# Sums of squares of the queries half a block later, and an inner dimension cut into two chunks of eleven tiles

## The chip, the cores and the metric

One core of one Trainium2 chip. The time is the device time of one execution in microseconds (us); less is better. Five engines run in parallel, each through its own instruction queue in order, and meet only at semaphores: TensorE (PE, with its weight loads PEld), VectorE (DVE), ScalarE (ACT), GpSimd (POOL) and SyncE (SP). In this kernel SP issues plain DMAs, POOL issues plain ones and ones that add to what is there.

## What is computed

Two layers of a streaming encoder on 16 + 512 tokens (528 columns), model width 1024, inner width 2816. Each layer: a SwiGLU, a mixer (a convolution branch and a windowed attention with 16 query and 4 key heads of 64, gated and summed), and a second SwiGLU.

```python
x = x + 0.5 * (silu(gate) * up) @ w_out          # gate | up = rms_norm(x) @ w_in, FFN 1
p = rms_norm(x) @ w_in                           # conv inputs | q | k | v | gates
q, k = rms_norm(q, q_norm), rms_norm(k, k_norm)  # over the 64 of each head
y_b = window_sink_attention(q, k, v, sinks) @ attn_w_out
x = x + (sigmoid(g_a) * conv_module(p) + sigmoid(g_b) * y_b) @ w_out
x = x + 0.5 * (silu(gate) * up) @ w_out          # FFN 2
```

## The kernel before, in words

**Precision.** Every weight and every activation is split in two float32r parts, high and low, and each product is made of three matmuls (high by high, high by low, low by high). The high part of a weight is a copy by ACT; the low part is either a subtraction by DVE, or ACT writes the negated high part and POOL adds the weights to it with an accumulating DMA.

**Four FFN stages** (s = 0 to 3, two in each layer; 22 inner tiles of 128 each; s = 3 runs on 512 columns, the others on two halves of 264). The input product of one inner tile, a "pair" of gate and up, is made by a seven-product scheme: P1 to P7, twelve matmuls each. TensorE's order for pair j is P1, P2, P7 of the pair before, P5, P6, P4 of the pair before, P3. DVE and ACT combine the products (L1532 to L1567) into `hh` and `hl`, the inner tiles.

**Chunks and output products.** `CHUNKS` cuts the 22 inner tiles into 7, 7 and 8. After the last pair of a chunk TensorE runs the output products: for each of 8 outputs m, the chunk's inner tiles times one block of `w_out`, accumulated in PSUM (`out_products`, L1127). Since P7 and P4 of the last pair still have to follow, the first block is begun with one inner tile, then comes P7, a second tile, P4 and the rest. The block of weights for an output goes through three slots in rotation: SP loads it (`load_out`, L544) when the slot's last user is done, ACT makes the high part (`out_hi`, L696), DVE the low part (`out_lo`, L1463), and TensorE waits for `ob_lo`. DVE then scales the output out of PSUM (L1634) and adds it to the residual (L1638). In the last chunk of a stage, what follows on the residual is done output by output as well: in stage 1 the operands of the next seven-product scheme (`x7_parts` on ACT, `x7_operands` on DVE, which end with L1396), in stages 0 and 2 the operands of the mixer.

**The slots.** The units that hold weights are shared by pairs, output blocks and mixer blocks; `freed`, `out_freed` and `mix_freed` say which product has to be over before a unit is loaded again. Pairs alternate between two sets of units, and the output blocks use the set that the last pair did not.

**The mixer.** Per layer four groups g of 11 blocks (two of queries, one of keys and values, eight others that fill TensorE while attention is prepared), each of 8 x 3 matmuls over the tokens (`products`, L1061). At the end of block 3 stands `head_stats`: 9 small products (8 in the second layer) of the squared queries with a two-column matrix (L1224), the keys' sums of squares (L1227), and transposes of the values (L1230 to L1233). ACT then takes the roots (`head_std`: L903 for the queries, L904 for the keys) and copies the transposed values (L906 to L908, which release `v_ready`); DVE takes reciprocals and scales the keys (`head_rms`, L1711 to L1723); SP copies the keys to the other half of the partitions (L570), and TensorE makes the first scores after block 5 (L1252). The queries' factors are first needed by `row_max`, which DVE reaches in block 5.

Of the kernel before, what the change touches and what calls it, by code (L numbers as in the profile page):

```python
# [29 lines left out]
P = 128  # L30
# [8 lines left out]
CHUNKS = ((0, 7), (7, 14), (14, KF))  # L39
# [46 lines left out]
OUT_UNITS = ((0, 2, 4), (8, 10, 12))  # L86
# [86 lines left out]
def tensor_order():  # L173

    for s in range(STAGES):
        for c, (a, b) in enumerate(CHUNKS):
            for j in range(s * KF + a, s * KF + b):
                yield "P1", j
                yield "P2", j
                if j > s * KF + a:  # L180
                    yield "P7", j - 1
                yield "P5", j
                yield "P6", j
                if j > s * KF + a:
# [4 lines left out]
            for m in range(KD):  # L189
                yield "out", s, c, m  # L190
        if s % 2 == 0:
            for n in range(NBLK):
                yield "mix", s // 2, n
# [5 lines left out]
def freed(j, part):  # L199

    s, c, i = chunk_of(j)
    product = {"A": "P2", "S12": "P6", "S43": "P7", "A22": "P4"}[part]
    if i > 1:
        return USED[product, j - 2]
    after_mixer = c == 0 and begins(s)
    if after_mixer and s == 0:
        return 0
    if after_mixer:
        m = {"A": 6, "S12": 7, "S43": 5, "A22": 4}[part]
        return USED["mix", s // 2, B_MO + m] if i or part == "A22" else 0  # L210
# [5 lines left out]
    return USED["out", s, c, {"A": 6, "S12": 7, "S43": 5}[part]]  # L216
# [32 lines left out]
def build(nc, x, params, qk_gain, sinks, pairs, outs7, outs8, mixes, out):  # L249
# [7 lines left out]
    with ctx:  # L257
# [47 lines left out]
        hh, hl = sb("hh", [P, KD, NT], F32R, ffn), sb("hl", [P, KD, NT], F32R, ffn)  # L305
# [112 lines left out]
        def out_block(s, c, m):  # L418

            last = s * KF + CHUNKS[c][1] - 1  # L420
            return (s * len(CHUNKS) + c) * KD + m + 1, OUT_UNITS[1 - REGION[last]][m % 3], CHUNKS[c][1] - CHUNKS[c][0]

        def out_load(s, c, m):

            return (s * len(CHUNKS) + c) * (3 if m % 3 < 2 else 2) + m // 3 + 1
# [46 lines left out]
        qk_stat = sem("qk_stat")  # L472
# [47 lines left out]
        def _(sp):  # L520
# [17 lines left out]
            def load_out(s, c, m):  # L538
                count, u, k = out_block(s, c, m)
                sp.wait_ge(blk_used, out_freed(s, c, m))  # L540
                n = count - 1 - (s * len(CHUNKS) + c) * KD
                i = s * len(CHUNKS) + c
                src = outs8[s * KD + n, :, :, :] if k == KD else outs7[(i - s) * KD + n, :, :, :]
                sp.dma_start(units(f32_units, u, 2)[:, 0:k, :], src).then_inc(ob_in[m % 3], 16)  # L544

            def stage(s):
                for c, (ta, tb) in enumerate(CHUNKS):
                    for t in range(ta, tb):
                        j = s * KF + t
                        if j + 2 < run_of(j)[1]:  # L550
                            load_pair(j + 2)
                        if t == tb - 2:
                            load_out(s, c, 0)
                        if t == tb - 1:
                            load_out(s, c, 1)
                            load_out(s, c, 2)
                    for m in range(KD - 3):
                        load_out(s, c, m + 3)
# [86 lines left out]
        def _(act):  # L645
# [45 lines left out]
            def out_hi(s, c, m):  # L691
                if m >= KD:
# [84 lines left out]
            def ffn(l, f):  # L777
                s = 2 * l + f
                last_chunk = len(CHUNKS) - 1
                for c, (ta, tb) in enumerate(CHUNKS):  # L780
# [56 lines left out]
                    for m in range(KD):  # L837
                        if m:
                            out_hi(s, c, m + 2)
                        if m == KD - 1 and more:  # L840
                            base_hi(j1 + 1)
                        if c == last_chunk:
                            if f == 0 and m == 0:
                                act.wait_ge(lay, l + 1)
                            if f == 0 and m in (5, 7):
                                neg(l, B_MIX + (m - 5) // 2)
                            act.wait_ge(res_done, out_block(s, c, m)[0])
                            outer(l, m, 1 if f == 0 else 3, R_MIX if f == 0 else None)
# [52 lines left out]
            def head_std(l, g):  # L901
                act.wait_ge(qk_stat, l * GROUPS + g + 1)
                func(qstd[:, lead(l):, :], qss[:, lead(l):, :], ACT.Sqrt, bias=eps64[:, :]).then_inc(qstd_ready, 1)  # L903
# [4 lines left out]
                func(vm[:, HD:P], pov[0:MB, 128:128 + HD], ACT.Copy).then_inc(v_ready, 1)  # L908

# [19 lines left out]
            for l in range(DEPTH):  # L929
                ffn(l, 0)  # L930

                for g in range(GROUPS):
# [23 lines left out]
                    h(4)  # L956
                    fill_tanh(l, g, 4)
# [86 lines left out]
        def _(pe):  # L1044
# [72 lines left out]
            def out_products(s, c, m, ks):  # L1117
                count, u, n = out_block(s, c, m)
                hi, lo = units(hi_units, u, 2), units(lo_units, u, 2)
                j0 = s * KF + CHUNKS[c][0]  # L1120
                post = s == STAGES - 1
                for k in ks:
                    if m == 0 and k >= n - 2:
                        pe.wait_ge(h_lo, j0 + k + 1)
                    for p, (a, b) in enumerate(((hi, hh), (hi, hl), (lo, hh))):
                        for h, t, width in pieces(post):
                            ins = mm(po[:, 2 * ps(m) + h, 0:width], a[:, k, :], b[:, k, t:t + width],  # L1127
                                     start=k == 0 and p == 0, stop=k == n - 1 and p == 2, skip_group_check=True)
                if n - 1 in ks:
                    ins.then_inc(blk_used, 1)  # L1130

            def ffn(l, f):
                s, which = 2 * l + f, 2 * f
                for c, (ta, tb) in enumerate(CHUNKS):
# [61 lines left out]
                    n = tb - ta  # L1196
                    pe.wait_ge(ob_lo, before_c + 1)
# [6 lines left out]
                    out_products(s, c, 0, range(2, n))  # L1204
                    for m in range(1, KD):
                        pe.wait_ge(ob_lo, before_c + m + 1)
                        if m > 1:
                            pe.wait_ge(ffn_taken, before_c + m - 1)
                        out_products(s, c, m, range(n))
# [7 lines left out]
            def head_stats(l, g):  # L1217
# [11 lines left out]
                for c in range(NCH):  # L1229
# [4 lines left out]
                    .then_inc(qk_stat, 1)  # L1234

# [56 lines left out]
            def mixer_in(l):  # L1292
                for g in range(GROUPS):
# [7 lines left out]
                    mids = {7: do(lambda: S(1)), 8: do(lambda: V(0), lambda: T(1)),  # L1301
# [67 lines left out]
        def _(dve):  # L1369
# [88 lines left out]
            def out_lo(s, c, m):  # L1458
                if m >= KD:
                    return  # L1460
# [109 lines left out]
            def ffn(l, f):  # L1570
                s = 2 * l + f
                post = s == STAGES - 1
                for c, (ta, tb) in enumerate(CHUNKS):
# [47 lines left out]
                    for m in range(KD):  # L1621
# [8 lines left out]
                        count = out_block(s, c, m)[0]  # L1630
                        dve.wait_ge(blk_used, USED["out", s, c, m])
# [76 lines left out]
            def head_rms(l, g):  # L1708
                n = l * GROUPS + g
                dve.wait_ge(qstd_ready, n + 1)  # L1710
                nc.vector.reciprocal(qrms[:, :, :], qstd[:, :, :]).then_inc(qrms_ready, 1)  # L1711
                dve.wait_ge(kstd_ready, n + 1)
                dve.wait_ge(qrms_ready, n + 1)
                ts(nqrms[:, :, :], qrms[:, :, :], -1.0, None, ALU.mult)
# [9 lines left out]
                    .then_inc(kn_ready, 1)  # L1724

# [46 lines left out]
            for l in range(DEPTH):  # L1772
# [10 lines left out]
                for g in range(GROUPS):  # L1783
                    for i in range(GB_N):
# [98 lines left out]
def laid_out(inputs):  # L1883
# [12 lines left out]
    for l in range(DEPTH):  # L1896
        for name in ("ffn1", "ffn2"):
# [3 lines left out]
            for a, b in CHUNKS:  # L1901
                outs += [block(f"{name}_w_out", l, a, b - a, ((m * P, P),)) for m in range(KD)]
# [10 lines left out]
        "outs7": np.stack([b for b in outs if b.shape[1] < KD]),  # L1913
        "outs8": np.stack([b for b in outs if b.shape[1] == KD]),
# [18 lines left out]
```

## Time and profile before

| | |
|---|---|
| median of 3 runs | 2423.99 us (2418.34 to 2425.91) |
| profiled execution: time | 2424.94 us |
| profiled execution: span | 2423.1 us |
| mean granted TensorE clock over the span | 0.992 |
| busy: PE, DVE, ACT, POOL | 98%, 71%, 50%, 14% |

The views that follow are the page's list of busy engines and of DMA issues, the list of TensorE's waits, sums over stretches (with the granted clock), the chain of waits and the order of time. "Busy" counts a matmul from its start to its end; since the next one starts before that, TensorE can lose time without being idle, and the starts in the order of time have to be compared. A matmul over 264 columns that follows another densely starts some 0.122 us after it, and ends 0.28 us after its start.

### The profile page before, as it was taken

To read this page: it belongs to the slowest core of one execution; us is meant where nothing else is said; L and a number is where in the kernel's file an instruction comes from. 1 tells how busy PE (TensorE), PEld (TensorE's weight loads), DVE (VectorE), ACT (ScalarE), POOL (GpSimd) and SP (SyncE) were. 2 spreads that over 40 slices of the span, in tenths; PEclk is the share of its full clock that TensorE was granted. 3 is DMA by queue.
4 is the path that set the end of the run, shared out by engine and by line. 5 is a ranking of instruction groups with operands and counts; after the bars stand their busy time and mean duration, and the time that the engine had idled before them with its cause. 6 is when DMAs were issued, how large, how long until landed. Compare 5 with 4: busy or idle time off the path is not lost.

```text
span 2423.1 us, 43031 instructions
## 1 busy us (share of the span) xinstructions
PE 2378.2 (98%) x17637; PEld 2236.9 (92%) x17637; DVE 1720.2 (71%) x2740; ACT 1222.0 (50%) x1991; POOL 345.3 (14%) x454
## 2 busy tenths in 40 slices
PE   7999999999999999999999999999999999999999
PEld 6999999999999999999989999998888777889897
DVE  8766664798886477667787676647888855867584
ACT  7554543443444375546565455543434454746371
POOL 1010101121112210101001101011211122101010
PEclk9999999999999999999999999999999999999999
DMA  6655646666667966556546556466676698657472
GB/s 172 154 136 147 154 111 140 145 146 144 139 141 172 209 134 152 145 144 155 146 106 161 141 145 151 112 146 145 145 153 144 130 217 191 144 143 175 116 176 92
DMA packets 106756, 358.69 MB, mean 148 GB/s; under 512 B 12096, under 2 KB 12096, under 8 KB 106560
## 3 DMA queue, kind: packets, MB, share of 16 engines
q0 software_dynamic: 64080, 210.53, 43.0%
q1 hardware_dynamic: 42112, 145.08, 19.8%
q8 instruction: 140, 2.29, 0.4%
q14 instruction: 56, 0.46, 0.1%
q10 hardware_dynamic: 368, 0.33, 0.0%
HBM read 351.41 MB, written 2.10 MB: 146 GB/s over the span
## 4 chain that ended last, share of the span: by engine, by line
PE 87%; DVE 4%; DMA 4%; ACT 3%; issue 2%; POOL 0%; DVEq 0%; ACTq 0%; SPq 0%
PE po L1061 30%; PE po L1078 20%; PE po L1127 19%; PE ptr L1078 8%; PE pov L1078 5%; DMA wla<-in_mixes 1%; PE pov L1289 1%; PE pov L1287 1%; PE ptr L1268 1%; PE pstat L1252 1%; DMA raw<-in_pairs 1%; PE pov L1224 1%; DVE rms L1520 0%; PE pstat L1227 0%; DMA wha<-in_mixes 0%
## 5 line engine op out<-in xcount | busy, mean ns | idle before, releaser
L1061 PE MATMUL po<-xh,wha 128*128 128x264 f32 (+1 forms) x1408 | 348.2, 314 | 4.5 <-DMA wla<-in_mixes 3.9
L1061 PE MATMUL po<-xl,wha 128*128 128x264 f32 (+1 forms) x1408 | 339.2, 308 | 0.0
L1061 PE MATMUL po<-xh,wla 128*128 128x264 f32 (+1 forms) x1408 | 338.4, 307 | 0.0
L1670 DVE SCALAR_TENSOR_TENSOR cv<-ub,lp,cv 128x528 f32<-128x528 f32 (+1 forms) x480 | 333.3, 754 | 1.7
L1061 PEld LDWEIGHTS po<-xh,wha 128*128 128x128 f32 x1408 | 230.3, 191 | 23.3 <-DVE t L1873 3.5
L1078 PE MATMUL po<-x7h,wha 128*128 128x264 f32 (+1 forms) x844 | 241.1, 286 | 4.1 <-ACT tmp L702 1.6
L1078 PE MATMUL po<-x7l,wha 128*128 128x264 f32 (+1 forms) x844 | 240.3, 285 | 0.0
L1061 PEld LDWEIGHTS po<-xh,wla 128*128 128x128 f32 x1408 | 229.7, 191 | 11.3
L1078 PE MATMUL po<-x7h,wla 128*128 128x264 f32 (+1 forms) x844 | 239.8, 284 | 0.0
L1061 PEld LDWEIGHTS po<-xl,wha 128*128 128x128 f32 x1408 | 229.7, 191 | 10.3
L658 ACT ACTIVATE wla<-wha 128x1024 fp32r<-128x1024 f32 x136 | 143.1, 1054 | 162.2 <-DMA wha<-in_mixes 162.1
L1078 PE MATMUL po<-x7h,whb 128*128 128x264 f32 (+1 forms) x692 | 197.8, 286 | 11.8 <-DMA wlb<-in_pairs 4.6
L1078 PE MATMUL po<-x7l,whb 128*128 128x264 f32 (+1 forms) x692 | 197.0, 285 | 0.0
L1078 PE MATMUL po<-x7h,wlb 128*128 128x264 f32 (+1 forms) x692 | 196.6, 284 | 0.0
L607 POOL DMA_DIRECT2D wha<-in_mixes x136 | 75.8, 560 | 674.8 <-PE po L1061 612.5
L1078 PEld LDWEIGHTS po<-x7h,wha 128*128 128x128 f32 x844 | 159.1, 189 | 5.6 <-issue 2.8
L1127 PE MATMUL po<-hh,wha 128*128 128x264 f32 (+1 forms) x688 | 161.7, 303 | 0.0
L1127 PE MATMUL po<-hh,wla 128*128 128x264 f32 (+1 forms) x688 | 161.3, 303 | 0.0
L1127 PE MATMUL po<-hl,wha 128*128 128x264 f32 (+1 forms) x688 | 161.2, 302 | 0.0
L1078 PEld LDWEIGHTS po<-x7l,wha 128*128 128x128 f32 x844 | 159.6, 189 | 0.0
L1078 PEld LDWEIGHTS po<-x7h,wla 128*128 128x128 f32 x844 | 159.3, 189 | 0.0
L611 POOL DMA_DIRECT2D wla<-in_mixes x136 | 122.4, 900 | 171.1 <-ACT wla L658 169.9
(247 smaller groups left out, 6297.0 us busy)
## 6 DMA issues: line engine op xcount, KB each, us to landing
wha<-in_mixes POOLq DMA_DIRECT2D x136, 512.0 KB, 4.4
wla<-in_mixes POOLq DMA_DIRECT2D x136, 512.0 KB, 6.4
raw<-in_pairs SPq DMA_DIRECT2D x88, 768.0 KB, 5.1
wlb<-in_pairs POOLq DMA_DIRECT2D x45, 512.0 KB, 7.6
raw<-in_pairs SPq DMA_DIRECT2D x88, 256.0 KB, 5.9
wla<-in_pairs POOLq DMA_DIRECT2D x87, 256.0 KB, 6.7
wfa<-in_outs SPq DMA_DIRECT2D x48, 448.0 KB, 3.4
wla<-in_pairs POOLq DMA_DIRECT2D x41, 512.0 KB, 8.2
```

The source lines that it names most:

```text
L607: pool.dma_start(mix_units(hi_units, n), mixes[l * NBLK + n, :, :, :]).then_inc(w_hi[n % 4], 16)
L611: pool.dma_start(mix_units(lo_units, n), mixes[l * NBLK + n, :, :, :], accum_op=ALU.add)\
L658: func(mix_units(lo_units, n), mix_units(hi_units, n).bitcast(F32), ACT.Copy, scale=-1.0)\
L1061: ins = mm(po[:, 2 * out_slot + h, 0:width], w[:, k, :], v[:, k, t:t + width], start=begin and k == 0 and p == 0, stop=last and k == kt - ...
L1078: ins = mm(bank, a[:, kp, :], b[:, kp, cols7], start=begin and kp == 0 and p == 0, stop=kp == KP - 1 and p == 2, skip_group_check=True)
L1127: ins = mm(po[:, 2 * ps(m) + h, 0:width], a[:, k, :], b[:, k, t:t + width], start=k == 0 and p == 0, stop=k == n - 1 and p == 2, skip_grou ...
L1224: mm(qss[:, pos, :], qsq[:, tok0(pos):tok0(pos) + CHUNK, :].rearrange("p n j -> p (n j)"), halves[:, :], start=True, stop=True)
L1252: ins = mm(score(i, h), q[r, :], kw[r, c:c + WK], start=True, stop=True)
L1268: tr(ptr[:, h * P:(h + 1) * P], pw[:, (b + 1) % 2, at:at + WIN], ident[:, :])
L1287: mm(dst[h * HD:(h + 1) * HD], vw[:, pos - 1, :], cut(pt[:, h, :]), start=True, stop=False, skip_group_check=True)
L1289: mm(dst, vm[:, :], cut(ptm[:, :]), start=pos == 0, stop=True, skip_group_check=True).then_inc(pv_done, 1)
L1670: stt(cv[:, j, a:], u, w, cv[:, j, a:], ALU.mult, ALU.add).then_inc(conv_step, 1)
```

## The change

The inner tiles are cut into two chunks of 11 in place of 7, 7 and 8, so each output is added to the residual twice per stage and not three times. An output's 11 tiles of weights no longer fit a slot of 8; they come as two blocks of 6 and 5 tiles, 16 blocks per chunk through the same three slots, in the order of units 2, 4, 0 where it was 0, 2, 4. The inner tiles `hh`, `hl` grow from 8 to 11 tiles, and the room for them comes from the scratch space that the software DMA queue reserves (`dynamic_dma_scratch_size=4096`). In the mixer the queries' small products, their root and their reciprocal leave `head_stats`, `head_std` and `head_rms`: TensorE makes them in the middle of block 4 after `v_ready`, ACT takes the root before that block's tanh, DVE the reciprocal after that block was taken.

```diff
-CHUNKS = ((0, 7), (7, 14), (14, KF))
+CHUNKS = ((0, 11), (11, KF))
+CHUNK_T = 11
+BLOCKS = ((0, 6), (6, CHUNK_T))
+NB = KD * len(BLOCKS)
-OUT_UNITS = ((0, 2, 4), (8, 10, 12))
+OUT_UNITS = ((2, 4, 0), (10, 12, 8))
...
 def out_freed(s, c, m):
     if m > 2:
         return USED["out", s, c, m - 3]
-    return USED[("P2", "P6", "P7")[m], s * KF + CHUNKS[c][1] - 2]
+    return USED[("P6", "P7", "P2")[m], s * KF + CHUNKS[c][1] - 2]
...
-    return USED["out", 2 * l, len(CHUNKS) - 1, n + 4]
+    return USED["out", 2 * l, len(CHUNKS) - 1, NB - 4 + n]
...
                     for m in range(KD):
                         if m:
-                            out_hi(s, c, m + 2)
+                            out_hi(s, c, 2 * m + 2)
+                        out_hi(s, c, 2 * m + 3)
...
             def head_std(l, g):
                 act.wait_ge(qk_stat, l * GROUPS + g + 1)
-                func(qstd[:, lead(l):, :], qss[:, lead(l):, :], ACT.Sqrt, bias=eps64[:, :]).then_inc(qstd_ready, 1)
...
+            def query_std(l, g):
+                act.wait_ge(q_stat, l * GROUPS + g + 1)
+                func(qstd[:, lead(l):, :], qss[:, lead(l):, :], ACT.Sqrt, bias=eps64[:, :]).then_inc(qstd_ready, 1)
...
                     h(4)
+                    query_std(l, g)
                     fill_tanh(l, g, 4)
...
+                    for b in range(NB):
+                        pe.wait_ge(ob_lo, before_b + b + 1)
+                        m = b // 2
+                        if m > 1 and b % 2 == 0:
                             pe.wait_ge(ffn_taken, before_c + m - 1)
+                        out_products(s, c, b, range(0 if b else 2, out_block(s, c, b)[2]))
...
                 pe.wait_ge(ksq_ready, l * GROUPS + g + 1)
-                pe.wait_ge(qsq_ready, 2 * (l * GROUPS + g) + 2)
                 pe.wait_ge(o_lo, (l * GROUPS + g) * NBAT + 1)
-                for pos in range(lead(l), NPOS):
-                    mm(qss[:, pos, :], qsq[:, tok0(pos):tok0(pos) + CHUNK, :].rearrange("p n j -> p (n j)"),
-                       halves[:, :], start=True, stop=True)
...
+            def query_stats(l, g):
+                pe.wait_ge(qsq_ready, 2 * (l * GROUPS + g) + 2)
+                pe.wait_ge(v_ready, l * GROUPS + g + 1)
+                for pos in range(lead(l), NPOS):
+                    ins = mm(qss[:, pos, :], qsq[:, tok0(pos):tok0(pos) + CHUNK, :].rearrange("p n j -> p (n j)"),
+                             halves[:, :], start=True, stop=True)
+                ins.then_inc(q_stat, 1)
...
-                    mids = {7: do(lambda: S(1)), 8: do(lambda: V(0), lambda: T(1)),
+                    mids = {4: do(lambda: query_stats(l, g)), 7: do(lambda: S(1)), 8: do(lambda: V(0), lambda: T(1)),
...
                         if m:
-                            out_lo(s, c, m + 2)
+                            out_lo(s, c, 2 * m + 2)
+                        out_lo(s, c, 2 * m + 3)
...
+            def query_rms(l, g):
+                n = l * GROUPS + g
+                dve.wait_ge(qstd_ready, n + 1)
+                nc.vector.reciprocal(qrms[:, :, :], qstd[:, :, :]).then_inc(qrms_ready, 1)
+                dve.wait_ge(qrms_ready, n + 1)
+                ts(nqrms[:, :, :], qrms[:, :, :], -1.0, None, ALU.mult)
...
                         if i == 3:
                             head_rms(l, g)
+                        if i == 4:
+                            query_rms(l, g)
...
-    nc = bacc.Bacc("TRN2", target_bir_lowering=False, num_devices=1)
+    nc = bacc.Bacc("TRN2", target_bir_lowering=False, num_devices=1, dynamic_dma_scratch_size=4096)
```

## Rows read from the trace of the kernel before

**Rows 1.** The page: each engine's busy time, share of the span, instructions.
```profile
PE 2378.2 (98%) x17637; PEld 2236.9 (92%) x17637; DVE 1720.2 (71%) x2740; ACT 1222.0 (50%) x1991; POOL 345.3 (14%) x454
```
**Rows 2.** TensorE's waits, whole span: us in total, times, longest us.
```profile
PE po L1078 <- ACT tmp L707: 2.6, 4, 0.9
...
PE po L1061 <- DMA wla<-in_mixes: 3.9, 4, 1.5
...
PE pstat L1252 <- DMA kw<-kw: 0.8, 1, 0.8
```
**Rows 3.** Sums over 10 us (a group's statistics; last: stage 2): busy (x), PEclk, DMA.
```profile
413.00:423.00 10.00, 10.00 (x72) 9.30 (x71) 6.11 (x7) 4.52 (x8) 1.44 (x2) 0.83 0.65 132
497.00:507.00 10.00, 10.00 (x84) 9.30 (x83) 6.48 (x8) 5.83 (x10) 1.44 (x2) 1.00 0.61 124
...
663.80:673.80 10.00, 10.00 (x59) 8.57 (x58) 5.12 (x6) 5.83 (x10) 1.44 (x2) 0.66 0.59 120
...
1236.00:1246.00 10.00, 7.17 (x31) 6.34 (x31) 8.15 (x13) 7.04 (x10) 0.86 (x1) 0.67 0.29 52
```
**Rows 4.** The same sums for TensorE alone, at either clock, after the first group's statistics.
```profile
417.00:420.00 3.00, 3.00 (x14) 0.50 0.91 173
420.40:423.40 3.00, 3.00 (x27) 1.00 0.02 4
```
**Rows 5.** Order of time, first group's statistics: start us, us, engine, line, [idle before].
```profile
413.05 2.07 PE L1224 MATMUL pov<-halves,pw 128*128 128x2 f32 x18
...
415.04 1.10 PE L1227 MATMUL pstat<-t,ones 64*64 64x264 f32 x4
...
416.68 0.22 PE L1233 MATMUL pov<-ident,kvp 64*32 64x64 f32 x1
...
417.24 0.27 DVE L1711 RECIPROCAL qrms<-qstd 128x18 f32<-128x18 f32 x1 [3.29 <-ACT qstd L903]
...
418.27 0.20 ACT L908 ACTIVATE vm<-pov 32x64 f32<-32x64 f32 x1
```
**Rows 6.** Order of time: second layer's query products; two idle stretches of TensorE.
```profile
1871.04 1.84 PE L1224 MATMUL pov<-halves,pw 128*128 128x2 f32 x16
...
2097.31 0.39 PE L1078 MATMUL po<-x7h,whb 128*128 128x256 f32 x1 [1.75 <-ACT tmp L702]
...
1240.27 0.59 PE L1078 MATMUL ptr<-x7h,wha 128*128 128x264 f32 x1 [2.29 <-DVE x7l L1419]
```
**Rows 7.** Order of time, end of stage 0's first chunk; last row: of its third.
```profile
98.96 1.08 DVE L1463 TENSOR_TENSOR wla<-wfa,wha 128x896 fp32r<-128x896 f32 x1
...
99.53 0.41 PE L1127 MATMUL po<-hh,wha 128*128 128x264 f32 x2
99.63 0.94 ACT L696 ACTIVATE wha<-wfa 128x896 fp32r<-128x896 f32 x1
...
100.53 0.36 PE L1078 MATMUL ptr<-x7h,whb 128*128 128x264 f32 x1
...
338.82 0.36 PE L1078 MATMUL ptr<-x7h,wha 128*128 128x264 f32 x1 [0.24 <-DVE tmp L1536]
```
**Rows 8.** DMA issues (KB, us to landing); and output products in the chain of waits.
```profile
raw<-in_pairs SPq DMA_DIRECT2D x88, 768.0 KB, 5.1
...
wfa<-in_outs SPq DMA_DIRECT2D x48, 448.0 KB, 3.4
...
104.66 39.46 PE po L1127 x324
```
**Rows 9.** Order of time, last outputs of stage 1 and start of stage 2.
```profile
1221.94 0.49 PE L1127 MATMUL po<-hh,whb 128*128 128x264 f32 x2 [0.48 <-DVE t L1634]
...
1233.74 0.28 PE L1078 MATMUL ptr<-x7h,wha 128*128 128x264 f32 x1
...
1235.83 0.70 DVE L1634 SCALAR_TENSOR_TENSOR t<-po,rms 128x528 f32<-128x528 f32 x1
...
1241.65 0.70 DVE L1396 TENSOR_TENSOR pw<-pw 128x528 f32<-128x528 f32 x1
```

More of the change, by code:

```diff
@@ L188, in tensor_order @@
             yield "P4", s * KF + b - 1
-            for m in range(KD):
-                yield "out", s, c, m
+            for b in range(NB):
+                yield "out", s, c, b
         if s % 2 == 0:
@@ L215, in freed @@
     s, c, _ = chunk_of(j - 2)
-    return USED["out", s, c, {"A": 6, "S12": 7, "S43": 5}[part]]
+    return USED["out", s, c, {"A": NB - 2, "S12": NB - 1, "S43": NB - 3}[part]]
 def out_freed(s, c, m):
@@ L304, in build @@
         raw = sb("raw", [P, 2, 4 * KP, P], at=ffn)
-        hh, hl = sb("hh", [P, KD, NT], F32R, ffn), sb("hl", [P, KD, NT], F32R, ffn)
+        hh, hl = sb("hh", [P, CHUNK_T, NT], F32R, ffn), sb("hl", [P, CHUNK_T, NT], F32R, ffn)
         ffn.close()
@@ L420, in out_block @@
             last = s * KF + CHUNKS[c][1] - 1
-            return (s * len(CHUNKS) + c) * KD + m + 1, OUT_UNITS[1 - REGION[last]][m % 3], CHUNKS[c][1] - CHUNKS[c][0]
+            a, b = BLOCKS[m % 2]
+            return (s * len(CHUNKS) + c) * NB + m + 1, OUT_UNITS[1 - REGION[last]][m % 3], b - a
         def out_load(s, c, m):
-            return (s * len(CHUNKS) + c) * (3 if m % 3 < 2 else 2) + m // 3 + 1
+            return (s * len(CHUNKS) + c) * len(range(m % 3, NB, 3)) + m // 3 + 1
         def mix_units(bufs, n):
@@ L471, in build @@
         qsq_ready, ksq_ready = sem("qsq_ready"), sem("ksq_ready")
-        qk_stat = sem("qk_stat")
+        qk_stat, q_stat = sem("qk_stat"), sem("q_stat")
         qstd_ready, kstd_ready, v_ready = sem("qstd_ready"), sem("kstd_ready"), sem("v_ready")
@@ L556, in stage @@
                             load_out(s, c, 2)
-                    for m in range(KD - 3):
-                        load_out(s, c, m + 3)
+                    for b in range(NB - 3):
+                        load_out(s, c, b + 3)
             load_x(0)
@@ L691, in out_hi @@
             def out_hi(s, c, m):
-                if m >= KD:
+                if m >= NB:
                     return
@@ L846, in ffn @@
                                 neg(l, B_MIX + (m - 5) // 2)
-                            act.wait_ge(res_done, out_block(s, c, m)[0])
+                            act.wait_ge(res_done, (s * len(CHUNKS) + c) * KD + m + 1)
                             outer(l, m, 1 if f == 0 else 3, R_MIX if f == 0 else None)
@@ L1115, in last_product, with out_products @@
                 seventh("P4", j, x_bank(j), begin=False)
-            def out_products(s, c, m, ks):
-                count, u, n = out_block(s, c, m)
+            def out_products(s, c, b, ks):
+                _, u, size = out_block(s, c, b)
                 hi, lo = units(hi_units, u, 2), units(lo_units, u, 2)
                 j0 = s * KF + CHUNKS[c][0]
+                m, k0 = b // 2, BLOCKS[b % 2][0]
                 post = s == STAGES - 1
                 for k in ks:
[L1123 to L1129, printed above, removed]
+                    t = k0 + k
+                    if m == 0 and t >= CHUNK_T - 2:
+                        pe.wait_ge(h_lo, j0 + t + 1)
+                    for p, (w, v) in enumerate(((hi, hh), (hi, hl), (lo, hh))):
+                        for h, x, width in pieces(post):
+                            ins = mm(po[:, 2 * ps(m) + h, 0:width], w[:, k, :], v[:, t, x:x + width],
+                                     start=t == 0 and p == 0, stop=t == CHUNK_T - 1 and p == 2,
+                                     skip_group_check=True)
+                if size - 1 in ks:
                     ins.then_inc(blk_used, 1)
@@ L1194, in ffn @@
                         seventh("P3", j, Z, begin=False)
-                    n = tb - ta
-                    pe.wait_ge(ob_lo, before_c + 1)
+                    before_b = (s * len(CHUNKS) + c) * NB
+                    pe.wait_ge(ob_lo, before_b + 1)
                     pe.wait_ge(c21_taken, j1 - 1)
@@ L1203, in ffn @@
                     last_product(j1 - 1)
[L1204 to L1207, printed above, removed]
+                    for b in range(NB):
+                        pe.wait_ge(ob_lo, before_b + b + 1)
+                        m = b // 2
+                        if m > 1 and b % 2 == 0:
                             pe.wait_ge(ffn_taken, before_c + m - 1)
-                        out_products(s, c, m, range(n))
+                        out_products(s, c, b, range(0 if b else 2, out_block(s, c, b)[2]))
             pe.wait_ge(const_done, CONSTS)
@@ L1458, in out_lo @@
             def out_lo(s, c, m):
-                if m >= KD:
+                if m >= NB:
                     return
@@ L1901, in laid_out @@
             for a, b in CHUNKS:
-                outs += [block(f"{name}_w_out", l, a, b - a, ((m * P, P),)) for m in range(KD)]
+                for m in range(KD):
+                    outs += [block(f"{name}_w_out", l, a + k, z - k, ((m * P, P),)) for k, z in BLOCKS]
         for n in range(NBLK):
@@ L1912, in laid_out @@
         "pairs": np.stack(pairs),
-        "outs7": np.stack([b for b in outs if b.shape[1] < KD]),
-        "outs8": np.stack([b for b in outs if b.shape[1] == KD]),
+        "outs6": np.stack(outs[0::2]),
+        "outs5": np.stack(outs[1::2]),
         "mixes": np.stack(mixes),
```

14 lines of the change are left out of this document (4 added, 10 removed).

## The prediction, made before the changed kernel ran

> **What bounds the kernel now.** I read the page first: TensorE is busy for 98% of the span, no other engine for more than 71% [rows 1]. So the time is TensorE's work, and the change keeps every matmul of it. What it can win is only what TensorE loses between matmuls, or by running them slowly. For that I read three views: TensorE's waits, which are few and short [rows 2]; the granted clock in stretches; and the order of time, because a matmul's start tells of a loss that "idle" hides.
>
> The clock is the larger finding. In the ten microseconds from a group's statistics on, it is 0.83 in three of the eight groups, 0.66 in two, 1.00 in three [rows 3]. A mean of 0.83 over 10 us is 3.4 us at 1.2 GHz, one of 0.66 is 6.8 us, together 3 x 3.4 + 2 x 6.8 = 23.8 us. At the lower level 14 matmuls start in 3 us, at 2.4 GHz 27 [rows 4], so a microsecond there loses 13/27 = 0.48 us: 11.4 us in all. I take 10.7, since part of the two long ones falls on the transposes. What TensorE did before each drop is the statistics: 2.07 us of products with two columns, 1.10 us of key sums and 0.7 us of transposes, up to 416.9 [rows 5]: 3.8 us with hardly a column streamed.
>
> **The change part by part. The query products.** The 2.07 us (1.84 in the second layer [rows 6]) move by half a block. TensorE's work is the same; the low stretch of 3.8 us becomes one of 1.8 us (from 415.04 to the end of the transposes) and one of 2.07 or 1.84 us with 2.9 us of dense matmuls between. Does the clock still drop? The nearest rows are idle stretches: 1.75 us with no drop of the clock, 2.29 us with one [rows 6, 3]. The key part and the second layer lie at the harmless row, the first layer's 2.07 us lies between. I take a drop in two of the four groups of the first layer, none in the second: 2 x 3.4 x 0.48 = 3.3 us. Bounds: none, and all eight (13.1 us). Net: 10.7 - 3.3 = **7.4 us less**.
>
> The keys' root no longer stands behind 2.07 us of products and the queries' root; DVE waits 3.29 us there now [rows 5]. The keys reach SP some 2 us sooner, and the one wait for their copy, 0.8 us [rows 2], goes: **0.8 less**. What the move adds: TensorE waits in mid block 4 for `v_ready`; all of that block is queued behind it. ACT's last copy ends 418.47, 1.6 us after the last transpose [rows 5], and less without the queries' root; mid block comes 24 x 0.122 = 2.9 us after it. So at nothing, under 1.3 us of cover; 8 x 0.5 us if ACT were half a microsecond later than that. ACT's root and its table loads stand in the wait for block 4, and DVE's 0.3 us reciprocal after the same block, needed only in block 5: nothing.
>
> **Fewer chunk ends.** There TensorE runs six matmuls of the first output block, then needs DVE's L1536 for P7. L1536 stands behind the low part of the second block (98.96 to 100.04). Six matmuls from 99.53 end their turn at 100.26; P7 starts at 100.53: 0.27 lost, with no idle shown. At a third chunk, whose blocks have 8 tiles, idle is 0.24, so the loss is about 0.39 [rows 7]. Now 8 x 0.27 + 4 x 0.39 = 3.7 us. Afterwards that block has 5 tiles: 5/7 of 1.08 is 0.77, 0.3 sooner, and P7 waits for P3's own combination, some 0.12: 8 x 0.12 = 1.0. **2.7 less.**
>
> But the second block's load moves from P6 to P7 of the pair before: from its issue to P7's turn are four products and six matmuls, 54 x 0.122 = 6.6 us. ACT takes 5/7 of 0.94 = 0.67, DVE 0.77, L1536 0.43, the steps between them some 0.4: the load may take 4.3 us. One of 448 KB takes 3.4, one of 768 KB 5.1 [rows 8]; this is 320 KB with 384 KB right behind. I take the first; the second would cost 0.8 at each of 8 ends, 6.4 us.
>
> **Fewer chunk starts.** A chunk's start refills the pipeline of weights; TensorE waits there for ACT L707 four times, 2.6 us [rows 2], in eight starts within stages. Four remain: **1.3 less** (0 to 2.6).
>
> **Within the outputs.** An output product runs at 39.46/324 = 0.122 us a matmul [rows 8], a chunk's outputs without a break. A slot is refilled while two other blocks run: 14 tiles x 6 x 0.122 = 10.2 us now, 11 tiles or 8.05 us afterwards. The refill takes 3.4 + 0.81 (ACT, 6/7 of 0.94) + 0.93 (DVE) + 0.5 = 5.6 us, hidden with 2.4 to spare.
>
> Where DVE has more to do it is not: in stage 1's last chunk an odd output costs DVE 1235.83 to 1242.35, 6.5 us [rows 9], and now the low part of the *next output's second* block stands ahead of it. That block is free after the current output's 6 tiles; load, ACT, DVE take 3.4 + 0.67 + 0.77 + 0.4 = 5.2 us, 1.6 after the output's end; plus 6.5, plus the next low part 0.93 and 0.1: 9.1 against 8.05. So 1.1 us for outputs 1, 3 and 5 (0.2 if the load shortens with its bytes); I take 0.7 x 3 = 2 us, and one stall of 0.6 [rows 9] goes: 1.4 more. On the other side DVE now starts the last output 2.1 us after TensorE ended it (1233.74 to 1235.83 [rows 9]), since six-microsecond outputs leave it behind; eight-microsecond ones do not. Stage 2's first pair resumes 1.8 us sooner, its idle 2.29 falls to about 1, and the drop there (0.67: 6.6 us, 3.2 lost [rows 3]) should go: 5.0, of which I let 1.5 be given back to ACT and the weights, late next. Net **2.1 less** (1.5 more to 4.5 less).
>
> **The mixer's first weights** come later in the first layer (the last pair now leaves the set that the mixer needs to the outputs). The second layer already works so. TensorE's four waits for `wla` are 3.9 us, at most 1.5 [rows 2]; I add **0.3** (0 to 1.5). The scratch for POOL's descriptors falls to 4096 bytes; no row shows POOL short of it. At nothing; if POOL had to wait for room, those 3.9 us could double.
>
> Sum: 7.4 + 0.8 + 2.7 + 1.3 + 2.1 - 0.3 = 14.0 from 2424.94, the profiled execution's time, 1 us above the median of the runs shown: 2411.
>
> One rule speaks against the change: the Trainium skill, "DMA: Bandwidth & Descriptors", section "Bandwidth", wants transfers of a megabyte and gives 0.95 us for 64 KB and 6.15 for 1 MB. Read as a line, an estimate by that page, an output's 11 tiles cost 2.7 + 2.3 = 5.0 us in two transfers, against 4.8 as 11/7 of one of 448 KB: over 64 outputs 17 us more of transfer, none of it TensorE's while the 8.05 us hold. The row for 448 KB, 3.4 us [rows 8], is 0.4 above that line.
>
> **The rivals.** *The clock drops as before.* If the clock falls after the two-column products of every group, eight drops lose 13.1 where 10.7 are lost now: 2424.94 - 6.6 + 2.4 = 2420.7. For it: the 2.29 us row is near. Against: 1.75 us is harmless, and the second layer's is 1.84.
> *No drop at all, and nothing lost in stage 1:* 2411 - 3.3 - 2 = 2405.7.
> *The output side gives nothing,* each gain taken back by shorter cover: only 7.4 + 0.8 stay, 2416.7.
> *Slower: the second block's load comes late.* Its ACT copy stands ahead of copies that P7 needs, its low part ahead of L1536. It costs time from a landing of 4.3 us on, and eats all of 15 us at 1.9 us per end, from 6.2 us on. At 7 us (above the row's 5.1 for more bytes) 8 x 2.7 us of waiting and, such idle being like the 2.29 us one, 8 x 1.6 us of lower clock: 2424.94 - 15 + 34 = 2444. Against: loads at the same place take 3.4 us.
> *The change not doing what it says* would be statistics that still run as one stretch; the 24 matmuls between speak against it.
>
> **How the numbers follow.** Forecast 0.50 (2411), no drop 0.17 (2406), nothing from the outputs 0.10 (2417), drops as before 0.15 (2421), late load 0.08 (2444). A measurement of this kernel tells some 0.3%, 7.3 us, from no change; 2416.7 is that edge, so the third case is halved: faster 0.72, same 0.20, slower 0.08. The range takes in the second and fourth case with the bounds: 2402 to 2421.
>
> **What would show it.** Clock 1.00 in the 10 us after most `head_stats`, with L1224 in mid block 4 and no wait before it; no wait for `kw`; P7 at a chunk's end within 0.15 us of its turn; four L707 waits become about two; stage 2's start without a drop, L1634 right behind the last output; waits of about 0.7 us before blocks 4, 8 and 12 of stage 1's second chunk. I am wrong if the clock drops after L1224 in every group, or if TensorE waits for `ob_lo` elsewhere.

## The result, and the profile after

The changed kernel takes 2400.89 us, the median of 4 runs (2399.2 to 2402.58), and the kernel before 2421.68 us beside it (4 runs, 2418.34 to 2425.91): a ratio of 0.9909, with a 95% interval of 0.9892 to 0.9926. The forecast was 2411, in a range of 2402 to 2421. The direction held and so did the two mechanisms with the largest terms, the clock and the chunk ends, but the gain by the medians, 20.8 us, is half as large again as the 14.0 of the forecast, and the time lies 1 us below the range. The profiled execution took 2400.89 us with a span of 2399.1 us, 24.0 us less than the profiled one of before, which was itself 3.3 us above its kernel's median.

The list of busy engines, answering [rows 1]: the count of matmuls is the same, and TensorE's share too.

```profile
PE 2359.5 (98%) x17637; PEld 2222.9 (93%) x17637; DVE 1681.3 (70%) x2708; ACT 1243.5 (52%) x2035; POOL 345.4 (14%) x454
```

TensorE's waits (us in total, times, longest), answering [rows 2]. The wait for `kw` is gone from the list, the four waits of a chunk's start on ACT are two (L710 is L707 of before), and the outputs have a new one, on DVE's low parts:

```profile
PE po L1086 <- ACT tmp L705: 5.3, 4, 1.8
...
PE po L1137 <- DVE wla L1478: 2.0, 3, 1.4
...
PE po L1069 <- DMA wla<-in_mixes: 1.6, 3, 1.1
...
PE po L1086 <- ACT tmp L710: 1.0, 2, 0.8
```

Sums over 10 us, answering [rows 3] (PEclk is the third column from the end): three of the eight groups from their key sums on, then the starts of stages 2 and 3. All eight groups read 1.00, and so does stage 2, which read 0.67; stage 3 reads 0.83.

```profile
407.60:417.60 10.00, 10.00 (x83) 9.29 (x83) 5.78 (x5) 4.66 (x8) 1.41 (x2) 1.00 0.67 144
...
572.90:582.90 10.00, 10.00 (x83) 9.30 (x83) 8.37 (x10) 8.27 (x11) 1.44 (x2) 1.00 0.69 145
...
1850.10:1860.10 10.00, 10.00 (x59) 8.12 (x59) 8.28 (x10) 8.35 (x11) 1.73 (x3) 1.00 0.72 147
1226.00:1236.00 10.00, 8.27 (x61) 7.51 (x60) 8.19 (x13) 8.12 (x12) 0.00 (x0) 1.00 0.27 64
2074.00:2084.00 10.00, 9.28 (x65) 9.28 (x66) 8.16 (x14) 7.04 (x12) 1.73 (x2) 0.83 0.90 184
```

The first group in order of time, answering [rows 5]: the key sums, ACT's last copy (which releases `v_ready`), the queries' products 1.6 us behind it with no wait before them, and the key copy on SP, 7.75 us after the group's small products began. The last row is the key copy of before, 10 us after the 413.05 of [rows 5].

```profile
407.63 1.10 PE L1234 MATMUL pstat<-t,ones 64*64 64x264 f32 x4
...
410.70 0.20 ACT L911 ACTIVATE vm<-pov 32x64 f32<-32x64 f32 x1
...
412.47 2.07 PE L1247 MATMUL pov<-halves,pw 128*128 128x2 f32 x18
...
415.38 0.53 SPq L573 DMA_DIRECT2D kw<-kw  x1
...
423.03 0.53 SPq L570 DMA_DIRECT2D kw<-kw  x1
```

**Where the time went.** Since "idle" hides most losses here, I add up losses from the starts: for each matmul, the distance to the next start less the median distance of the same operation and width in the kernel before (0.122 us for 264 columns). Summed by place, for the two profiled executions, in us:

| place | before | after | change | forecast |
|---|---|---|---|---|
| mixers, at the lower clock | 10.9 | 0.0 | -10.9 | -7.4 |
| mixers, other losses | 12.6 | 13.4 | +0.8 | -0.5 |
| chunk ends, P7 and P4 | 6.5 | 0.9 | -5.7 | -2.7 |
| chunk starts within a stage | 5.0 | 1.7 | -3.2 | -1.3 |
| last outputs of stage 1, start of stage 2 | 10.5 | 8.6 | -1.9 | -2.1 |
| all other outputs | 2.2 | 0.2 | -2.0 | 0 |
| first 60 us of the program | 11.7 | 9.6 | -2.1 | 0 |
| starts of stages 1 and 3 | 10.3 | 11.9 | +1.6 | 0 |
| other pairs | 1.7 | 1.1 | -0.6 | 0 |
| sum | 71.4 | 47.3 | -24.1 | -14.0 |

### The profile page after: what moved, and what is told of

Same layout as the page of the kernel before. It is cut to its first block, busy times and chain, and to the rows that moved or that the text cites. A ratio compares the mean times of both kernels' runs of the same rounds, so it can differ in the third digit from the quotient of the medians.

```text
span 2399.1 us, 43012 instructions
## 1 busy us (share of the span) xinstructions
PE 2359.5 (98%) x17637; PEld 2222.9 (93%) x17637; DVE 1681.3 (70%) x2708; ACT 1243.5 (52%) x2035; POOL 345.4 (14%) x454
## 3 DMA queue, kind: packets, MB, share of 16 engines
q8 instruction: 140, 2.29, 0.4%
## 4 chain that ended last, share of the span: by engine, by line
PE 90%; DVE 3%; ACT 3%; DMA 2%; issue 2%; POOL 0%; DVEq 0%; ACTq 0%; SPq 0%
PE po L1069 31%; PE po L1086 22%; PE po L1137 20%; PE ptr L1086 7%; PE pov L1086 5%; PE pov L1304 1%; PE pov L1302 1%; PE ptr L1283 1%; PE pstat L1267 1%; DMA wha<-in_mixes 1%; PE pov L1247 1%; DMA wla<-in_mixes 1%; DVE rms L1535 0%; ACT x7h L748 0%; DMA wfa<-in_outs 0%
## 5 line engine op out<-in xcount | busy, mean ns | idle before, releaser
L1137 PE MATMUL po<-hh,wha 128*128 128x264 f32 (+1 forms) x1232 | 282.7, 299 | 2.0 <-DVE wla L1478 2.0
L1137 PE MATMUL po<-hl,wha 128*128 128x264 f32 (+1 forms) x1232 | 283.7, 300 | 0.0
L1137 PE MATMUL po<-hh,wla 128*128 128x264 f32 (+1 forms) x1232 | 283.7, 300 | 0.0
L1478 DVE TENSOR_TENSOR wla<-wfa,wha 128x768 fp32r<-128x768 f32 (+1 forms) x128 | 113.7, 890 | 201.6 <-ACT wha L699 201.5
L699 ACT ACTIVATE wha<-wfa 128x768 fp32r<-128x768 f32 (+1 forms) x128 | 101.0, 789 | 266.5 <-DMA wfa<-in_outs 266.3
L1086 PE MATMUL po<-x7h,whb 128*128 128x264 f32 (+1 forms) x768 | 221.9, 289 | 16.1 <-ACT tmp L705 5.3
L1086 PE MATMUL po<-x7h,wlb 128*128 128x264 f32 (+1 forms) x768 | 218.7, 285 | 0.0
L1137 PEld LDWEIGHTS po<-hh,wha 128*128 128x128 f32 x1232 | 196.1, 188 | 10.5 <-DVE wla L1478 2.6
L1137 PEld LDWEIGHTS po<-hh,wla 128*128 128x128 f32 x1232 | 196.9, 189 | 7.5
L1137 PEld LDWEIGHTS po<-hl,wha 128*128 128x128 f32 x1232 | 196.4, 188 | 7.6
```

What stands on the lines that cost most here:

```text
L1086: ins = mm(bank, a[:, kp, :], b[:, kp, cols7], start=begin and kp == 0 and p == 0, stop=kp == KP - 1 and p == 2, skip_group_check=True)
L1137: ins = mm(po[:, 2 * ps(m) + h, 0:width], w[:, k, :], v[:, t, x:x + width], start=t == 0 and p == 0, stop=t == CHUNK_T - 1 and p == 2, ski ...
L1478: tt(units(lo_units, u, 2)[:, 0:k, :], units(f32_units, u, 2)[:, 0:k, :], units(hi_units, u, 2)[:, 0:k, :].bitcast(F32), ALU.subtract).the ...
```

## The experiments

The theory after the result had two halves: the clock falls after small products in one stretch of 3.8 us and not after the two stretches that the change makes of it; and a chunk's end loses what DVE's low parts delay, at P7 and at P4. The first four runs test the first half and the sum of the parts, the other four the second half and what is left.

**The queries alone.** The mixer part of the diff, applied to the kernel before:

```diff
-                    mids = {7: do(lambda: S(1)), 8: ...
+                    mids = {4: do(lambda: query_stats(l, g)), 7: do(lambda: S(1)), 8: ...
```

> The kernel before with the mixer part alone: the queries' products, root and reciprocal half a block later, the chunks of 7, 7 and 8 as they were. Theory (the clock falls after 3.8 us of small products in one stretch, and not after 2 us of them between dense matmuls, whatever the chunks are): no drop of the clock in any of the eight groups, 10.9 us of lost matmul time gone, the wait for kw (1.0 us) gone too, 10 to 13 us less than before. The rival from the prediction (2 us are enough in the first layer): drops in two or more groups of the first layer, 7 to 9 us less. A second rival (the drops went because the new chunks moved the groups in time): drops stay in three or more groups, less than 6 us gained.

Measured: 2413.04 us, ratio 0.9956 (0.9941 to 0.9971). Ten microseconds from the queries' products on, for the first two groups; the other six read 1.00 too:

```profile
415.00:425.00 10.00, 10.00 (x86) 10.00 (x85) 4.66 (x8) 3.26 (x4) 1.44 (x2) 1.00 0.70 138
497.70:507.70 10.00, 10.00 (x86) 10.00 (x85) 9.93 (x17) 5.45 (x7) 1.44 (x2) 1.00 0.65 142
```

No group shows a drop, with the old chunks. The gain by the ratio, 10.7 us of 2422.5, is what the theory gave; in the profiled execution the mixers' loss at the lower clock is 0 where it was 10.9.

**The chunks alone.** The changed kernel with the queries' products, root and reciprocal back ahead of the keys'.

```diff
-                    mids = {4: do(lambda: query_stats(l, g)), 7: do(lambda: S(1)), 8: ...
+                    mids = {7: do(lambda: S(1)), 8: ...
```

> The changed kernel with the queries' products, root and reciprocal back where they were, ahead of the keys' sums: the chunk part alone. Theory: drops of the clock after three to six of the eight groups, as before; losses at the chunk ends near 0.8 us in all instead of 6.5, in-stage chunk starts about 2 us instead of 5, stage 1 to stage 2 about 2 us less, the rest of the gain in the outputs themselves: 9 to 13 us less than before. The prediction's own sum for this part was 6.1 less. If the two parts help each other, both this run and the one with the queries alone stay well below their shares, and their sum below 20.

Measured: 2411.00 us, ratio 0.9948 (0.9933 to 0.9963). Of the eight groups four drop, as in these three rows:

```profile
490.50:500.50 10.00, 10.00 (x72) 9.30 (x71) 6.47 (x9) 5.41 (x9) 1.44 (x2) 0.83 0.64 133
574.50:584.50 10.00, 10.00 (x59) 8.64 (x58) 5.31 (x7) 6.00 (x10) 1.44 (x2) 0.66 0.67 125
...
1693.80:1703.80 10.00, 10.00 (x46) 7.80 (x45) 5.97 (x8) 5.90 (x10) 1.44 (x2) 0.66 0.61 128
```

So the drops belong to the one stretch, and new chunks do not remove them. The chunk part is worth 12.6 us by the ratio, not the 6.1 of my sum. The two parts add up: 10.7 + 12.6 = 23.3, where the changed kernel gained 20.8 beside them and 22.0 at first, each within some 3.6 us.

**The changed kernel again**, without an edit.

> The changed kernel once more, to see what varies between executions. Theory: none of the eight groups shows a drop again; the drop at the start of the program (3.4 us long in the first look, 6.8 in the kernel before) and the one at the start of stage 3 may come or go, some 1.5 us each; ratio to before 0.990 to 0.9925. If the mixer's drops are a matter of chance, one or two of the eight groups show one here.

Measured: 2403.39 us, ratio 0.9914 (0.9899 to 0.9929); no group drops. Over the seven executions with the queries split and made once, that is 56 groups without a drop; with one stretch it was 5 of 8 in the kernel before and 4 of 8 above. The first 60 us lost 11.5 us here, as in the kernel before, and 9.6 in the first execution: the 2.1 us of the table's seventh line are chance. In the same way the two executions with three chunks lost 5.0 and 3.2 us at the chunk starts, and the six with two chunks of blocks of 6 and 5 lost 1.5 to 3.2 (mean 2.0).

**The queries' products twice.**

```diff
-                for pos in range(lead(l), NPOS):
+                for pos in 2 * tuple(range(lead(l), NPOS)):
                     ins = mm(qss...
```

> The changed kernel with the queries' two-column products in mid block 4 made twice (36 in a group of the first layer, 32 in the second; the second pass writes the same sums again), so 4.1 and 3.7 us of them in one stretch. Own cost: 136 more products of 0.112 us, 15.2 us. Theory (length of the stretch without dense work decides): the clock falls after most of the groups again, 1.5 or 3 us each, so 24 to 34 us more than the changed kernel. Rival (the drops belonged to the place, behind block 3 with the key sums and transposes, not to the length): no drops, 15 to 17 us more.

Measured: 2431.29 us, ratio 1.0035 (1.0024 to 1.0046), 27.9 more than the changed kernel beside it, where the products alone would make 15.2. Every group drops now; the first two, from the queries' products on:

```profile
413.20:423.20 10.00, 10.00 (x75) 10.00 (x74) 3.87 (x7) 2.92 (x4) 1.10 (x2) 0.83 0.31 64
499.40:509.40 10.00, 10.00 (x62) 10.00 (x61) 6.94 (x10) 4.28 (x5) 0.00 (x0) 0.66 0.35 71
```

The mixers lose 19.9 us at the lower clock. With the 15.2 that would be 35; in this profiled execution the first 60 us, the mixers' other losses, the chunk starts and the start of stage 3 (no drop here) lost some 7 us less than in the changed kernel's second one. The place in mid block 4 protects nothing: TensorE is 100% busy in both kernels, and what differs is how long it made products of two columns (3.6 to 4.9 us where it was 1.8 to 2.1) before the dense ones came back.

**Blocks of 3 and 8.**

```diff
-BLOCKS = ((0, 6), (6, CHUNK_T))
+BLOCKS = ((0, 3), (3, CHUNK_T))
```

> The changed kernel with an output's 11 tiles cut into blocks of 3 and 8 in place of 6 and 5. Theory (what delays P7 at a chunk's end is the work on the second block that stands ahead of P3's combination on DVE): the second block's load has 512 KB in place of 320, its copy on ACT takes some 1.06 us in place of 0.74, its low part 1.22 in place of 0.82, and P7 starts 0.8 to 1.7 us after its turn in place of 0.05: 6 to 14 us more than the changed kernel, all of it at the eight chunk ends. Rival (the wait at a chunk's end was that of three chunks' worth of other work, and the block's size does not matter): chunk ends stay near 0.9 us in all, time within 3 us of the changed kernel. The output products themselves should not wait: 8.05 us of cover for a refill.

**Blocks of 5 and 6.**

```diff
-BLOCKS = ((0, 6), (6, CHUNK_T))
+BLOCKS = ((0, 5), (5, CHUNK_T))
```

> The changed kernel with blocks of 5 and 6 tiles in place of 6 and 5. Theory: at a chunk's end DVE's low part of the second block ends just as P3's combination may start, with no time to spare, so one tile more (0.13 us on DVE, 0.1 on ACT, 64 KB) delays P7 by 0.15 to 0.5 us per end: 1 to 4 us more in all. Rival (size does not matter): the same as the changed kernel within 1 us at the chunk ends.

The end of stage 0's first chunk in order of time. In the changed kernel the second block's low part has 640 columns; its end decides when DVE takes P3 (L1551), and that when P7 (the last row) starts:

```profile
137.09 0.74 ACT L699 ACTIVATE wha<-wfa 128x640 fp32r<-128x640 f32 x1 [2.41 <-DMA wfa<-in_outs]
...
137.57 0.42 DVE L1576 TENSOR_TENSOR tmp<-tmp 128x264 f32<-128x264 f32 x1
...
137.91 0.82 DVE L1478 TENSOR_TENSOR wla<-wfa,wha 128x640 fp32r<-128x640 f32 x1
...
138.68 0.43 DVE L1551 TENSOR_TENSOR tmp<-po,tmp 128x264 f32<-128x264 f32 x1
...
138.97 0.40 PE L1137 MATMUL po<-hh,wla 128*128 128x264 f32 x2
...
139.26 0.37 PE L1086 MATMUL ptr<-x7h,whb 128*128 128x264 f32 x1
```

The same with blocks of 3 and 8:

```profile
137.07 1.06 ACT L699 ACTIVATE wha<-wfa 128x1024 fp32r<-128x1024 f32 x1 [2.00 <-DMA wfa<-in_outs]
...
137.96 0.42 DVE L1576 TENSOR_TENSOR tmp<-tmp 128x264 f32<-128x264 f32 x1
...
138.30 1.22 DVE L1478 TENSOR_TENSOR wla<-wfa,wha 128x1024 fp32r<-128x1024 f32 x1
...
139.44 0.43 DVE L1551 TENSOR_TENSOR tmp<-po,tmp 128x264 f32<-128x264 f32 x1
...
140.01 0.36 PE L1086 MATMUL ptr<-x7h,whb 128*128 128x264 f32 x1 [0.24 <-DVE tmp L1551]
```

And with blocks of 5 and 6:

```profile
137.80 0.42 DVE L1576 TENSOR_TENSOR tmp<-tmp 128x264 f32<-128x264 f32 x1
...
138.14 0.95 DVE L1478 TENSOR_TENSOR wla<-wfa,wha 128x768 fp32r<-128x768 f32 x1
...
139.20 0.40 PE L1137 MATMUL po<-hh,wla 128*128 128x264 f32 x2
...
139.58 0.36 PE L1086 MATMUL ptr<-x7h,whb 128*128 128x264 f32 x1
```

The two matmuls of L1137 start at 138.97 and 139.09 in the first case, so P7's turn is 139.21: it is 0.05 late. With 6 tiles it is 0.14 late, with 8 tiles 0.40. The kernel before had 7 tiles and 0.27, and 0.40 at its third chunk with 8 [rows 7]. One line goes through all of them, some 0.12 us a tile above 5, about what a tile costs DVE (0.82, 0.95, 1.22 us for 5, 6 and 8). In all three cases the low part starts 0.34 us after DVE's own L1576, and ACT's copy has ended by then (at 137.83, 138.13 and 137.43), so neither the load nor the copy set its start: its length on DVE is the mechanism at P7. P4's loss fits the same account with the third block: 0.04 to 0.05 us in stage 0 with 3, 5 or 6 tiles there, 0.15 with the 7 of before and 0.30 with its 8.

My expected sizes were too large, 6 to 14 us for 8 tiles and 1 to 4 for 6. At this end ACT starts its copy of 512 KB 3.9 us after SP's issue at 133.22, and that of 320 KB 4.3 us after the issue at 132.83, so the larger load came no later. All chunk ends together lose 3.7 us with 8 tiles, 1.6 with 6, 0.9 in the changed kernel. The times are 2402.19 (ratio 0.991, 0.9895 to 0.9925) and 2400.24 us (0.9904, 0.9889 to 0.9918), beside 2400.07 for the changed kernel, differences within the noise; the distances between starts are what shows the ends. What the ends lose comes back in stage 1's last outputs, where the waits fall from 2.8 us to 0.9 and 1.2, most likely since the first block of the next output is the smaller one.

**Two orders mended.** In stage 1's last chunk the next output's first block goes ahead of stage 2's operands, on ACT and DVE; and in a stage's third pair ACT copies P1 before it waits for the sum.

```diff
-                        if m:
+                        early = f == 1 and c == last_chunk and more
+                        if m and not (early and m % 2 == 0):
                             out_hi(s, c, 2 * m + 2)
                         out_hi(s, c, 2 * m + 3)
+                        if early and m % 2:
+                            out_hi(s, c, 2 * m + 4)
...
+                            if m % 2:
+                                out_lo(s, c, 2 * m + 4)
                             x7_operands(lw, 0, s + 1, m)
...
+                        third = j == s * KF + 2
+                        if third:
+                            copy_e1(j)
                         if j + 1 < j1:
                             sum_hi(j + 1, 0)
-                        copy_e1(j)
+                        if not third:
+                            copy_e1(j)
```

> The changed kernel with two orders mended. (1) In the last chunk of stage 1, ACT's and DVE's work on the next output's first block goes ahead of the operands of stage 2 instead of behind them: the three waits of the output products (1.5, 0.4 and 0.5 us) should go, 2.4 us. (2) In the third pair of a stage ACT copies P1 out of its bank ahead of the high part that waits for DVE instead of behind it: TensorE's wait ahead of that pair's P6 (1.8 us in each of stages 1, 2 and 3) should go, 5.4 us, and with it the drop of the clock at the start of stage 3 (1.5 us). Together 7 to 9 us less than the changed kernel; rival: the second is given back ahead of the next pair's products, since the high part comes 0.4 us later, and 3 to 5 us are left.

What the first edit acts on is in the changed kernel: DVE ends the operands of one odd output (L1411) and only then makes the low part for which TensorE waits.

```profile
1180.84 0.70 DVE L1411 TENSOR_TENSOR pw<-pw 128x528 f32<-128x528 f32 x1
1181.45 1.69 DVE L1478 TENSOR_TENSOR wla<-wfa,wha 128x768 fp32r<-128x768 f32 x2
...
1182.46 0.51 PE L1137 MATMUL po<-hh,wha 128*128 128x264 f32 x2 [1.37 <-DVE wla L1478]
```

Measured: 2396.02 us, ratio 0.988 (0.9863 to 0.9896), 4 us less than the changed kernel beside it and the fastest of all kernels here. That is the rival's 3 to 5 us and not the 7 to 9 of the theory. TensorE's waits with the new orders:

```profile
PE po L1093 <- DVE wla L1477: 1.9, 4, 0.6
...
PE po L1093 <- ACT tmp L705: 0.2, 1, 0.2
```

The outputs wait no longer for a low part (by starts 0.3 us are left of 2.8). The wait on ACT that was 5.3 us is 0.2, but the rival was right about part of it: TensorE then waits for DVE's low parts of the next pair (L1477, new in the list). By starts, each of the three stages wins back 0.8 us of 1.8. The clock at the start of stage 3 reads 1.00, as it did in four of nine executions that had the stop, so this one execution does not show that the edit did it. It has a drop of 3.4 us elsewhere, late in the second layer's mixer, behind a stop as long as the one that was mended:

```profile
2026.26 0.63 PE L1076 MATMUL po<-mh,wha 128*128 128x512 f32 x1 [1.75 <-DVE resid L1681]
```

**The changed kernel a third time**, beside these.

> The changed kernel a third time, beside the runs with other blocks and orders. Theory: no drop of the clock in any of the eight groups; the drop at the program's start is 3.4 or 6.8 us long by chance; starts of the second chunks lose 1.5 to 3 us in all, which varies with the arrival of weights.

Measured: 2400.07 us, ratio 0.9903 (0.9888 to 0.9918). No drop in a group. Stage 2's start, at 1.00 in the first execution, drops here, after an idle stretch of 1.2 us that was as long in the first:

```profile
1228.00:1238.00 10.00, 9.59 (x60) 0.83 0.23 80
```

## Why the prediction was too high, step by step

**The clock: the mechanism was right, the term 3.3 should have been 0.** The step that failed is "a drop in two of the four groups of the first layer". I put the first layer's 2.07 us of products between two idle stretches, 1.75 us without a drop and 2.29 us with one, and took the middle. The bracket was no bracket. The stop of 1.75 us that I called harmless [rows 6] stands in nine of the ten profiled executions and was followed by a drop in five, the changed kernel's among them (the row of stage 3 above), for 1.5 us each; the 2.07 us of products were followed by none in 28 groups of the first layer. One execution of a row tells what can happen, not what always does, and an idle stretch is not the same as a stretch of small products. The rival with no drop gave 2405.7 and had the chance 0.17; the one with all eight drops is refuted by the queries alone. The loss at the lower clock was well sized (10.7 for 10.9).

**The chunk ends: one stop counted where there are two.** The sum for P7 held: 3.7 us by the prediction, 3.9 by the starts, and 0.4 afterwards against 1.0. But P4, one tile later, stops in the same way, behind the *third* block's low part, and I had no term for it. The rows of before show it plainly, some 0.15 us between P4's turn, 0.122 after the second start of L1127 at 102.69, and its start at 102.97:

```profile
101.39 1.09 DVE L1463 TENSOR_TENSOR wla<-wfa,wha 128x896 fp32r<-128x896 f32 x1
...
102.39 0.43 DVE L1551 TENSOR_TENSOR tmp<-ptr,tmp 128x264 f32<-128x264 f32 x1
...
102.56 0.41 PE L1127 MATMUL po<-hh,wla 128*128 128x264 f32 x2
...
102.97 0.36 PE L1078 MATMUL ptr<-x7h,wha 128*128 128x264 f32 x1
```

Over the twelve ends P4 lost 2.6 us, now 0.4. That the block has 5 and 6 tiles in place of 7 was thus worth 5.7 us, not 2.7.

**The late load** did not cost, but it was near (in that rival 15 us are taken off, where the sum makes 14.0). At the first chunk end SP issues the second block at 132.83 and ACT starts its copy at 137.09, 4.3 us later, which is the break-even of the prediction; the usual is 2.9. P7 was 0.05 to 0.07 us late all the same, at all eight ends.

**Chunk starts:** 1.3 was the waits alone; by the starts the kernel before lost 5.0 in its profiled execution and 3.2 with the queries alone. The change is worth about 2 us here, within my bounds, and the rest of the 3.2 is how long the weights took in two executions.

**Stage 1 to stage 2** came out as summed, -1.9 for -2.1, with its parts: outputs wait 2.0 us in idle time as forecast, though before blocks 6, 10 and 14 and not 4, 8 and 12 (the low part stands behind the odd output's operands, so it is the output after that waits). L1650 follows the last output's end within 0.1 us. The drop is less likely, not gone: it was there in both executions with three chunks, and in eight with two chunks it came back once.

**The other outputs** are the one gain that no step named. The chain of waits has them as

```profile
143.27 62.57 PE po L1137 x516
```

which is 0.1213 us a matmul where it was 0.1218 [rows 8]. With the queries alone it stayed 0.1218, so it belongs to the chunks; within a chunk the same positions are slow by the same few ns in each output. Half a nanosecond over some 3,700 matmuls makes the 2 us. What sets it I did not settle.

**What was costed at nothing** held. There was no wait ahead of the queries' products, with 1.6 us of cover for 1.3 forecast. The key copy comes 7.75 us after the group's small products begin, where it took 10 us, and the wait for it is gone. POOL's descriptors had room enough: the mixer's low parts land in 6.5 us, as before in 6.4. The mixers' other losses ran from 11.6 to 15.9 us over these executions, whichever part of the change was in (the waits for `wla` alone made 1.6 us in the first execution of the changed kernel and 6.3 in the third), so 0.8 more says nothing. The listed blocks of 384 and 320 KB take 3.1 and 2.9 us from issue to landing, and the cover of 8.05 us hid them everywhere but in stage 1's last chunk, where the wait is DVE's (L1478). The estimate by the Trainium skill, "DMA: Bandwidth & Descriptors", section "Bandwidth", was 5.0 us of transfer for the two blocks; the 6.0 measured here are more than that page's line, whose figures leave out the issuing.

**The range** failed because its lower end had no room for what was most wrong. It is the rival with no drop, 2405.7, less 3.7 us, as much as the bounds of the chunk starts (1.3) and of stage 2 (2.4) make together; the stop at P4, the outputs and the first 60 us stood in it with nothing. The chunk ends and the clock together were 6.5 us off, and the outputs and the first 60 us another 4; all pointed the same way. The start of the sum added to it: the profiled 2424.94 is 3.3 us above the median of the four runs, and from that median the lower end would have been near 2399 and the time inside it, by luck, with the same terms wrong.

## What to carry to other kernels

Where an engine is 98% busy, look for its losses in the distances between starts, at every place where its stream hands over, and count each stop there: stops of 0.15 to 0.46 us, two at each of a dozen places and mostly with no idle shown, made 6.5 us, more than any wait in the list but the one at the program's start. When work that streams hardly a column has to run between dense matmuls, splitting it so that dense work lies between the parts can save the clock for nothing; test the length by doubling it. And a row from one execution gives a bound only if the same row has been seen in several.

## What was not expected of the hardware

At the start of stage 3 the third pair waits some 1.75 us for ACT in nine executions; five show the clock fall behind that stop, four do not. The sums over 10 us from there, in the kernel before (1.00) and in the changed kernel's second execution (0.83, as in the first):

```profile
2095.00:2105.00 10.00, 8.25 (x70) 1.00 0.86 185
```

```profile
2078.00:2088.00 10.00, 9.91 (x71) 0.83 0.90 192
```

The mixer's stop of the last edit's execution stands in the changed kernel's first one too, as long, and no drop followed it there (the 10 us from it read 1.00):

```profile
2029.24 0.50 PE L1069 MATMUL po<-mh,wha 128*128 128x512 f32 x1 [1.75 <-DVE resid L1671]
```

The third pair's wait in stages 1 and 2 is some 1.65 us long in the same nine executions, and none of these 18 stops was followed by a drop. So what the clock does behind a given stop differs between executions, while 2.07 us of two-column products never made it fall in 28 groups, and twice as many did in every one of eight. Whether the moment or what stands around the stop decides for the single stop was not tried.
